# The first mixer's output product as seven half-size block products, with block sums on GpSimd

## The reference, cut to what matters

```python
merged = jax.nn.sigmoid(gate_a) * (y_a @ w_up_a[i]) + jax.nn.sigmoid(gate_b) * (y_b @ w_up_b[i])
x = x + merged @ w_out[i]          # (512 x 1024) @ (1024 x 1024)
h = rmsnorm(x, g_ffn[i])
x = x + hier_moe(h, w_grp[i], w_exp[i], w1[i], w3[i], w2[i])
```

## Time and profile before

| | |
|---|---|
| median of 3 runs | 1656.4 us (1656.12 to 1660.41) |
| the profiled execution | 1658.27 us, span 1656.6 us |
| PE busy | 1642.8 us, 99% of the span |
| DVE, ACT, POOL busy | 63%, 43%, 7% |
| chain that ended last | PE 96% |
| `g_out` on PE | from 281.81 us to about 326.2 us |

### The profile page before, as it was taken

One profiled execution on the slowest core, in us unless ns is written; L12 is line 12 of the kernel. 1 busy time (PEld: TensorE's weight loads), 2 busy tenths in 40 slices (PEclk: granted clock), 3 DMA queues, 4 the chain that ended last, 5 costly groups with the idle time before them and its releaser, 6 DMA issues.

```text
span 1656.6 us, 25306 instructions
## 1 busy us (share of the span) xinstructions
PE 1642.8 (99%) x10312; PEld 1240.0 (75%) x10312; DVE 1044.9 (63%) x1373; ACT 718.4 (43%) x911; POOL 123.2 (7%) x175
## 2 busy tenths in 40 slices
PE   9999999999999999999999999999999999999998
PEld 7899998864545535554688877788888889889986
DVE  6989778453243334324578746567675577878887
ACT  6576553421101101111366533344643367757775
POOL 4000100000000000000111022210020000000000
PEclk9999999999999999999999999999999999999999
DMA  7132324888999999999551232124366527467864
GB/s 269 63 112 92 103 77 169 350 334 338 424 412 430 428 427 430 429 427 428 226 178 42 91 102 77 52 77 133 110 222 167 145 93 209 106 185 220 206 141 126
DMA packets 93697, 358.28 MB, mean 216 GB/s; under 512 B 8016, under 2 KB 8032, under 8 KB 81312
## 3 DMA queue, kind: packets, MB, share of 16 engines
q1 hardware_dynamic: 81264, 330.67, 52.0%
q0 software_dynamic: 12336, 26.23, 8.1%
HBM read 349.54 MB, written 7.34 MB: 215 GB/s over the span
## 4 chain that ended last, share of the span: by engine, by line
PE 96%; DVE 2%; DMA 1%; ACT 0%; issue 0%; POOL 0%; DVEq 0%; POOLq 0%; ACTq 0%
PE bank L3467 31%; PE bank L3896 13%; PE bank L4341 9%; PE bank L3630 9%; PE bank L4316 9%; PE bank L3909 7%; PE bank L3801 4%; PE bank L3842 3%; PE bank L4075 2%; PE bank L3492 2%; PE bank L3513 1%; DMA w_stage<-in_w_proj_gla 1%; PE bank L4105 1%; PE bank L4128 1%; PE bank L4175 1%
## 5 line engine op out<-in xcount | busy, mean ns | idle before, releaser
L3467 PE MATMUL bank<-act_hi,w_hi 128*128 128x512 f32 x544 | 215.5, 396 | 2.1 <-DVE gs_fm L2557 1.7
L3896 PE MATMUL bank<-ring,xgT 128*64 128x512 f32 x992 | 215.9, 592 | 0.6 <-ACT xgT L1641 0.6
L3467 PE MATMUL bank<-act_hi,w_lo 128*128 128x512 f32 x544 | 212.1, 390 | 0.0
L3467 PE MATMUL bank<-act_lo,w_hi 128*128 128x512 f32 x544 | 211.8, 389 | 0.0
L3896 PEld LDWEIGHTS bank<-ring,xgT 128*64 128x64 f32 x992 | 71.9, 137 | 140.2 <-issue 140.0
L1336 ACT ACTIVATE w_hi<-w_stage 128x2048 fp32r<-128x2048 f32 x50 | 95.9, 1919 | 138.9 <-PE bank L3467 128.7
L2249 DVE TENSOR_TENSOR w_lo<-w_stage,w_hi 128x2048 fp32r<-128x2048 f32 x50 | 115.2, 2303 | 62.9 <-ACT w_hi L1336 61.3
L4341 PE MATMUL bank<-down,part_hi 128*128 128x512 f32 x448 | 138.2, 390 | 0.1
L3467 PEld LDWEIGHTS bank<-act_hi,w_hi 128*128 128x128 f32 x544 | 102.1, 188 | 26.1 <-issue 2.8
L1671 ACT ACTIVATE y_hi_sb<-bank,slot_tables 128x512 fp32r<-128x512 f32 x32 | 22.0, 687 | 225.6 <-PE bank L3909 224.2
L3467 PEld LDWEIGHTS bank<-act_hi,w_lo 128*128 128x128 f32 x544 | 102.1, 188 | 21.8
(11 more groups left out here) (600 smaller groups left out, 3782.8 us busy)
## 6 DMA issues: line engine op xcount, KB each, us to landing
ring<-in_w SPq DMA_DIRECT2D x93, 2048.0 KB, 14.5
w_stage<-in_w_in SPq DMA_DIRECT2D x39, 1024.0 KB, 5.2
w_stage<-in_w_ff SPq DMA_DIRECT2D x19, 1024.0 KB, 6.3
b_sum<-in_w_ff POOLq DMA_DIRECT2D x12, 1024.0 KB, 10.9
w_stage<-in_w_out SPq DMA_DIRECT2D x8, 1024.0 KB, 5.7
b_one<-in_w_ff SPq DMA_DIRECT2D x6, 1024.0 KB, 7.0
stage<-in_w_ff SPq DMA_DIRECT2D x5, 1024.0 KB, 5.6
x_tm<-in_x SPq DMA_DIRECT2D x8, 512.0 KB, 9.4
```

The source lines that it names most:

```text
L3467: ins = pe.matmul(banks[j][:, :], left, right, start=(kc == 0 and k == 0 and n_pass == 0), stop=(kc == g.chunks - 1 and k == g.ktiles - 1 ...
L3896: ins = pe.matmul(dst[mine, :], xgT[:, 4 * kh + k, slots], up_weights(2 * w + kh, q, k, ahead), start=(kh == 0 and k == 0), stop=(kh == 1 ...
```

## The change

The 512 x 1024 by 1024 x 1024 product is cut into 2 x 2 blocks and made from seven products of half size (256 x 512 by 512 x 512) in place of eight. This needs sums and differences of blocks, of the weights (`o_t2`, `o_t3`, `o_t4`, and `o_b12` less `w_stage[1]`) and of the activations (`out_sum`), and each summed block is split into a high and a low part like any other. The four weight sums, the low part of `o_t2`, and the low parts of the weight operands of products 4 and 6 are made by GpSimd; the activation sums and the other low parts by VectorE; all high parts by ScalarE. A product adds its result to what the bank already holds where that is wanted, and VectorE adds two banks to `x` after each product. Two blocks of `w_out` get places of their own (`o_b12`, `o_b22`) and are loaded ahead; the ring's first loads come in the order 5, 4, 0, 3, 1, 2, and the gain comes later, since `o_s2` lies on its page.

```diff
-    g_out = Gemm(g_upb, 2, 2, "dve")
+    g_out = Gemm(g_upb, 1, PARTS + 1, "dve", tiles=2 * PARTS)
...
+        out_bank = (mb[0:2], mb[2:4], mb[2:4], mb[2:4], gb[2:4], mb[2:4], gb[2:4])
+        out_first = (True, True, False, False, True, False, False)
...
+        OUT_PLACES = ((2, 0), (2, 0), (2, 1), (0, 1), (0, 1), (0, 0), (2, 1))
...
+        out_split = {0: 0, 1: 1, 3: 2, 4: 3, 5: 4, 6: 5}
...
-            load_units(g_out, A["w_out"][0], 0)
-            load_gain(1, A["g_ffn"][0])
+            w_out = A["w_out"][0]
+            load_chunk(g_out.chunk0, 0, w_out, slice(0, 512), 0)
+            sp.wait_ge(y_lo, 2 * NH)
+            for dst, rows in ((o_b12, 512), (o_b22, 0)):
+                sp.dma_start(dst[:, :, :], w_out[rows:rows + 512, 512:D].rearrange("(k p) n -> p k n", p=P))\
+                    .then_inc(out_far, 16)
+            load_chunk(g_out.chunk0 + 1, 1, w_out, slice(0, 512), 1)
...
+            sp.wait_ge(out_sums, O_T3)
             sp.dma_start(route_f[:, :, 0:NG], A["w_grp"][0].rearrange("(k p) n -> p k n", p=P))\
                 .then_inc(route_in, 16)
             sp.dma_start(route_f[:, :, NG:ROUTED], A["w_exp"][0].rearrange("(k p) n -> p k n", p=P))\
                 .then_inc(route_in, 16)
-            sp.wait_ge(y_lo, AT_MERGED + KT)
-            for m in range(2):
-                load_half(m, 0)
-            sp.wait_ge(w_lo_done, split_count(g_out.chunk1 - 1))
+            load_half(5, 0)
+            sp.wait_ge(merged, KT)
+            load_half(4, 0)
+            sp.wait_ge(w_lo_done, split_count(out_chunk(1)))
+            for i in range(2):
+                sp.sem_inc(w_loaded[i], 48)
+            sp.wait_ge(out_sums, O_T1)
             sp.dma_start(early_p[:, :, :], A["p"]).then_inc(early_in, 16)
             sp.dma_start(early_ple[:, :, :], A["w_ple"][0][:, 0:HALF].rearrange("(k p) n -> p k n", p=P))\
                 .then_inc(early_in, 16)
-            for m in range(2, 6):
-                load_half(m, 0)
-            sp.wait_ge(pe_tiles, 4 * g_out.chunk1)
+            sp.wait_ge(w_lo_done, split_count(out_chunk(4)))
+            sp.wait_ge(pe_tiles, out_product(2))
+            load_half(0, 0)
+            sp.wait_ge(merged_sums, O_S4)
+            load_gain(1, A["g_ffn"][0])
+            sp.wait_ge(pe_tiles, out_product(4))
             for q in range(2):
                 sp.dma_start(extra[1][q][:, :, :].rearrange("p k n -> p (k n)"),
                              half_of(1, 1)[:, :, q, :, :].rearrange("o p k n -> p (o k n)")).then_inc(extra_in, 16)
+            sp.wait_ge(merged_low, OL_S4)
+            load_half(3, 0)
+            sp.wait_ge(pe_tiles, out_product(5))
+            load_half(1, 0)
+            sp.wait_ge(pe_tiles, 4 * g_out.chunk1)
+            load_half(2, 0)
...
+            pool.wait_ge(out_far, 32)
+            pool.tensor_tensor(o_t3[:, :, :], o_b22[:, :, :], o_b12[:, :, :], ALU.subtract).then_inc(out_sums, 1)
+            pool.wait_ge(w_loaded[1], ((g_out.chunk0 + 1) // 2 + 1) * 16)
+            pool.wait_ge(out_sums, O_T3)
+            pool.tensor_tensor(o_t2[:, :, :], o_t3[:, :, :], w_stage[1][:, :, :], ALU.add).then_inc(out_sums, 1)
+            pool.wait_ge(w_loaded[0], (g_out.chunk0 // 2 + 1) * 16)
+            pool.wait_ge(out_sums, O_T2)
+            pool.tensor_tensor(o_t4[:, :, :], w_stage[0][:, :, :], o_t2[:, :, :], ALU.subtract).then_inc(out_sums, 1)
+            pool.wait_ge(merged_high, OH_T2)
+            pool.wait_ge(out_sums, O_T4)
+            pool.tensor_tensor(o_t2_lo[:, :, :], o_t2[:, :, :], o_t2_hi[:, :, :].bitcast(F32), ALU.subtract)\
+                .then_inc(out_sums, 1)
+            pool.tensor_tensor(o_b12[:, :, :], o_b12[:, :, :], w_stage[1][:, :, :], ALU.subtract).then_inc(out_sums, 1)
+            for n, lo, raw, hi, parts in ((4, w_lo[1], o_b12, w_hi[1], 1), (6, o_b22_lo, o_b22, o_b22_hi, 3)):
+                pool.wait_ge(w_hi_done, split_count(out_chunk(n)))
+                pool.wait_ge(w_lo_done, split_count(out_chunk(n) - 1))
+                pool.tensor_tensor(lo[:, :, :], raw[:, :, :], hi[:, :, :].bitcast(F32), ALU.subtract)\
+                    .then_inc(w_lo_done, parts)
...
+            split_hi(out_chunk(0), 0)
+            act.wait_ge(pe_tiles, 4 * g_upa.chunk1)
+            for k in range(4):
+                act.wait_ge(merged, k + 1)
+                act.activation(act_hi[:, k, :], ga_fm[:, k, :], ACT.Copy).then_inc(y_hi, 1)
+            act.wait_ge(out_sums, O_T2)
+            act.activation(o_t2_hi[:, :, :], o_t2[:, :, :], ACT.Copy).then_inc(merged_high, 1)
+            split_hi(out_chunk(1), 1)
+            act.wait_ge(pe_tiles, 4 * g_upb.chunk1)
+            act.wait_ge(merged, KT)
+            act.activation(act_hi[:, far_k, far_t], ga_fm[:, far_k, far_t], ACT.Copy).then_inc(y_hi, 4)
+            act.wait_ge(pe_tiles, out_product(0))
+            act.wait_ge(merged_sums, O_S2)
+            act.activation(act_hi[:, near_k, far_t], o_s2[:, :, :], ACT.Copy).then_inc(merged_high, 1)
+            act.wait_ge(out_sums, O_T3)
+            act.activation(w_hi[0][:, :, :], o_t3[:, :, :], ACT.Copy).then_inc(w_hi_done, 1)
+            act.wait_ge(merged_sums, O_S3)
+            act.activation(act_hi[:, far_k, near_t], ga_fm[:, far_k, near_t], ACT.Copy).then_inc(merged_high, 1)
+            act.wait_ge(pe_tiles, out_product(1))
+            act.wait_ge(out_sums, O_T1)
+            act.activation(w_hi[1][:, :, :], o_b12[:, :, :], ACT.Copy).then_inc(w_hi_done, 1)
+            act.activation(act_hi[:, far_k, far_t], ga_fm[:, near_k, near_t], ACT.Copy).then_inc(merged_high, 1)
+            act.wait_ge(pe_tiles, out_product(2))
+            act.activation(o_t4_hi[:, :, :], o_t4[:, :, :], ACT.Copy).then_inc(w_hi_done, 1)
+            act.wait_ge(w_lo_done, split_count(out_chunk(3)))
+            act.activation(o_b22_hi[:, :, :], o_b22[:, :, :], ACT.Copy).then_inc(w_hi_done, 3)
...
+            for t in (2, 3):
+                act.wait_ge(out_dve, out_added(1, t - 2))
+                own.did(half_square(first_half(t), t, ssq))
...
+            act.wait_ge(pe_tiles, out_product(4))
+            act.wait_ge(merged_sums, O_S4)
+            act.activation(act_hi[:, far_k, far_t], ga_fm[:, near_k, far_t], ACT.Copy).then_inc(merged_high, 1)
...
-                split_lo(g_out.chunk0 + u, u)
-                for k in range(4 * u, 4 * u + 4):
-                    dve.wait_ge(y_hi, AT_MERGED + k + 1)
-                    rest(act_lo[:, k, :], ga_fm[:, k, :], act_hi[:, k, :]).then_inc(y_lo, 1)
+                if u == 0:
+                    split_lo(out_chunk(0), 0)
+                    for k in range(4):
+                        dve.wait_ge(y_hi, AT_MERGED + k + 1)
+                        rest(act_lo[:, k, :], ga_fm[:, k, :], act_hi[:, k, :]).then_inc(y_lo, 1)
+            m22, m12 = ga_fm[:, near_k, near_t], ga_fm[:, near_k, far_t]
+            m21, m11 = ga_fm[:, far_k, near_t], ga_fm[:, far_k, far_t]
+            def out_sum(dst, left, right, op):
+                dve.tensor_tensor(dst, left, right, op).then_inc(merged_sums, 1)
+            def out_low(k, t, src, high):
+                dve.wait_ge(merged_high, high)
+                rest(act_lo[:, k, t], src, act_hi[:, k, t]).then_inc(merged_low, 1)
+            def out_weights_low(n, lo, raw, hi):
+                dve.wait_ge(w_hi_done, split_count(out_chunk(n)))
+                rest(lo[:, :, :], raw[:, :, :], hi[:, :, :]).then_inc(w_lo_done, 1)
+            def out_add(n, j):
+                dve.wait_ge(pe_tiles, out_product(n, j))
+                if n in (1, 4, 6):
+                    dve.wait_ge(out_dve, out_added({1: 0, 4: 3, 6: 2}[n], j))
+                t, u = OUT_PLACES[n]
+                xt = x[:, t + j, u * 512:(u + 1) * 512]
+                dve.tensor_tensor(xt, xt, out_bank[n][j][:, :], ALU.add).then_inc(out_dve, 1)
+            dve.wait_ge(merged, KT)
+            out_sum(m22, m21, m22, ALU.add)
+            split_lo(out_chunk(1), 1)
+            dve.wait_ge(y_hi, AT_MERGED + KT)
+            rest(act_lo[:, far_k, far_t], m11, act_hi[:, far_k, far_t]).then_inc(y_lo, 4)
+            dve.wait_ge(merged_sums, O_S1)
+            out_sum(o_s2[:, :, :], m22, m11, ALU.subtract)
+            dve.wait_ge(rows_again, 16 + 16 * NT)
+            out_add(0, 0)
+            out_low(near_k, far_t, o_s2[:, :, :], OH_S2)
+            out_add(0, 1)
+            out_sum(m21, m11, m21, ALU.subtract)
+            out_add(1, 0)
+            out_weights_low(3, w_lo[0], o_t3, w_hi[0])
+            out_add(1, 1)
+            out_low(far_k, near_t, m21, OH_S3)
+            out_add(2, 0)
+            out_low(far_k, far_t, m22, OH_S1)
+            out_add(2, 1)
+            out_add(3, 0)
+            out_add(3, 1)
+            out_sum(m12, m12, o_s2[:, :, :], ALU.subtract)
+            dve.wait_ge(w_lo_done, split_count(out_chunk(4)))
+            out_weights_low(5, o_t4_lo, o_t4, o_t4_hi)
+            out_add(4, 0)
+            out_add(4, 1)
```

(68 more changed lines are left out.)

46 lines of the change are left out of this document (27 added, 19 removed).

## The result

| | before | after |
|---|---|---|
| median | 1656.55 us (1656.12 to 1660.41, 4 runs) | 1674.72 us (1674.02 to 1676.82, 4 runs) |
| profiled execution | 1658.27 us, span 1656.6 | 1675.17 us, span 1673.3 |

The changed kernel is slower: ratio 1.0107, 95% interval [1.0089, 1.0124], 18.2 us between the medians. 1673 was predicted.

The account below looks back on a forecast made before the run. TensorE, busy for 99% of the span, was taken as the bound: 5.4 us of matmuls saved, 21.7 of waits added, transposes and logits 7.8 for 7.1, so +16.9 on 1656.4: 1673, range 1658 to 1681.

Parts of the forecast that it names:

- The rival without meetings: In the `g_out` stage, GpSimd is slower but not in VectorE's way: 2.9 us earlier, median 1653.5, chance 0.15.
- A meeting: VectorE instruction with two SBUF inputs beside a GpSimd operation reading SBUF: held until GpSimd ends, about 4.4 us at most.
- Which operations meet: Before the first `g_out` tile: three branch sums and two `act_lo` held, first tile at 294.84, a wait of 13.0 us.
- Product 1: Second of the seven half-size products: starts at 304.7 after TensorE waits 4.4 us for VectorE's operands.
- the paragraph on the clock: After the 13 us wait, TensorE may run product 0 slower; 2.4 us if half does, absorbed by product 1's wait.
- I add 0: Lower TensorE clock after the long wait: nothing added to the forecast, up to 3 us at the high end.
- Product 3: Fourth half-size product: GpSimd's `w_lo[1]` for product 4 holds up VectorE; starts at 319.2 against 316.0, 3.15 us.
- The seventh operation: GpSimd's last added operation, 328.9 to 333.5: falls where VectorE waits for product 4's banks.
- row 2 would be late: At the stage's end: row 2 is 0.7 us late, so transposes and logits take 7.8 us in place of 7.1.
- Partway: GpSimd lets VectorE in partway, holding it 1.1 to 2.3 us each time: 1657 to 1664, about 1661, chance 0.13.
- DVE's back-to-back operations keep GpSimd out: In the `g_out` stage, two GpSimd operations enter later: 1.4 us less, 1671.9; counted with the forecast, together 0.66.
- The prediction's 1651.0: Median if even the new order of work costs nothing and the whole 5.4 us of saved matmuls come.

Follow-up runs that it names:

- fills: The changed kernel with each of GpSimd's seven sums and low parts replaced by memsets of the same tile, about as long, reading nothing from SBUF: 1653.69 us.
- the kernel before with five sums: The kernel before plus five GpSimd additions of 128x2048 on spare buffers: 1666.93 us with one tile as both inputs, 1672.54 with two tiles.
- matmuls in the wait: The changed kernel plus 60 unread matmuls of 128 columns on TensorE, issued before it waits for the first `g_out` operands: 1673.40 us.
- in quarters: The changed kernel with each of GpSimd's seven operations written as four of 128x512: 1666.05 us.

## Why the prediction was right, step by step

**Outside the meetings: right.** The rival without meetings was put at 1653.5; the kernel that takes the reads away is that rival, and it took 1653.69. Matmuls saved, waits of the new order, prefetches without cost are all in this one number. No wait of TensorE on a DMA stands in the stage of either kernel.

**A meeting lasts to GpSimd's end: right.** 4.4 us was taken for a meeting from GpSimd's start on; rows of after show 3.6, 3.7, 4.4, and 4.3 twice. The release came 0.14 us before GpSimd's recorded end, for 0.13 taken from the earlier trace rows. The Trainium skill ("SBUF — State Buffer", section "Who interferes with whom") also says that a GpSimd instruction that only writes doesn't contend with VectorE's two inputs, and that issue order decides who blocks. The trace agrees with both: no cost with fills, and GpSimd held for 1.7 us where `w_lo` had started first.

**Which operations meet: off by one place, at a price of 1.1 us.** The far blocks were to land near 266 and landed at 268.0. Branch sum 1 got away; branch sums 2 and 3, `w_lo` and two `act_lo` were met, in place of three sums and two `act_lo`. Five meetings either way, and the first tile at 295.97 for 294.84.

**Product 1: right in its start, wrong in its wait.** It started at 305.87 for 304.7. Its wait was 1.49 and not 4.4, because product 0 ran twelve distances at 0.427 us and a first of 0.56, 2.8 us more in all, and the wait took them up as the paragraph on the clock had it. "I add 0" held, and would have failed in a stage without a second wait: the kernel before with five sums paid for its slow distances. What the prediction read from the earlier trace rows they don't show: the granted clock is 1.00 of full speed in every stretch from 0 to 12 us, while the four matmuls took 2.04 us as while they took 1.08. The two levels are seen in the changed kernel, 0.50 with distances of 0.427 us and 1.00 with 0.227.

**Product 3: right.** 2.91 for 3.15, through the meeting that was named, at 320.41 for 319.2.

**The seventh operation meets nobody: wrong, without effect.** It met S4's low part (3.36 for 1.22), which had the room.

**The sum: 1.3 us too small, and the profiled execution hides it.** Predicted +16.9 to the logits' end, read +17.8 (351.24 less 333.43); the medians differ by 18.2. That the profiled execution came to 1675.17 for 1675.2 is luck. Before's profiled execution had a wait further on that the others don't have. PE's waits of before, whole kernel, then of after:

```profile
PE bank L3467 <- DVE gs_fm L2557: 1.7, 1, 1.7
```

```profile
PE bank L3610 <- DVE gs_fm L2657: 0.6, 1, 0.6
```

The kernels of the experiments show 0.3 to 0.8 there. The 1.1 us that before's execution lost at that place made up for the 0.9 missing from the sum and more.

The 0.9 is two errors that partly cancel. The first tile started 1.1 us later than worked out, products 1 and 3 1.2 later, and the last tile ended at 344.0 for 342.5, 1.5 later. The transposes and logits then took 7.2 us, as before, and not 7.8: that row 2 would be late had no effect there. For the first 1.1 the later landing is the likely cause, since with matmuls in the wait GpSimd started 0.68 us earlier and product 1 0.64 earlier; no run changes the landing alone.

**The rivals.** Partway (1661) fell with the first meeting, which was held to the end. That DVE's back-to-back operations keep GpSimd out fell for the sums of this stage: `o_b` at 289.14 entered between the four `act_lo`, and in quarters it did so at each of them. It stands for the rows that it was taken from. POOL and DVE of the kernel after, at the place of the earlier trace rows:

```profile
36.53 7.08 POOL L1266 TENSOR_SCALAR_AFFINE_SELECT w_spT<-w_spT 128x1024 f32<-128x1024 f32 x1 [3.48 <-DMA ln_b<-in_gm_ln_b]
```

```profile
37.75 4.90 DVE L2364 TENSOR_TENSOR act_lo<-xT,act_hi 128x512 fp32r<-128x512 f32 x8
```

In all ten profiled kernels this select begins at another moment, lasts 3.7 to 7.3 us and ends 0.95 to 0.97 us after the last of the eight `act_lo`, which take 4.90 us each time, as if nobody were there. So here VectorE's list did keep GpSimd out, while the two selects of 128x512 in the earlier trace rows held `act_lo`. What decides this is open; no run varies it.

**A better version.** None found. The fills show what this order of the work would bring if no meeting cost anything: 2.9 us, 0.2%. The prediction's 1651.0, without any wait, was reached by no run. With all sums on VectorE it is 4.4 us slower than before.
